# Small fp32 products of a state space mixer moved into tiles of the TensorE array, and a norm's last rows finished in pairs

## What is computed

```python
# even layer: [S5 complex-diagonal SSM (64 groups) | FoX forgetting attention (8 heads) | memory cross-attention (4 heads)]
# odd layer:  [latent attention (8 heads) | native sparse attention (8 heads) | memory cross-attention (4 heads)]
# h = h + W_out . concat_i( branch_i(RMSNorm(h)) * silu(gate_i) ), inputs and gates from ONE projection; one final RMSNorm

def s5_mixer(u, lam_re, lam_im, log_dt, b_re, b_im, c_re, c_im, d_skip, w_glu):
    ...
    bu_re = jnp.einsum('gpc,blgc->blgp', bb_re, uf)
    bu_im = jnp.einsum('gpc,blgc->blgp', bb_im, uf)
    ...
    _, _, xr, xi = lax.associative_scan(combine, (a_re, a_im, bu_re, bu_im), axis=1)
    y = (jnp.einsum('gcp,blgp->blgc', c_re.astype(f32), xr)
         - jnp.einsum('gcp,blgp->blgc', c_im.astype(f32), xi)
         + d_skip.astype(f32) * uf).reshape(B_, L, S5_WIDTH)
    z = jax.nn.gelu(y)
    z = z * jax.nn.sigmoid(z @ w_glu.astype(f32))

def rms_norm(x, g):
    y = xf * lax.rsqrt(jnp.mean(xf * xf, axis=-1, keepdims=True) + RMS_EPS)
```

## Time and profile before

| | |
|---|---|
| median of three runs | 2323.07 us (2321.97 to 2323.17) |
| profiled execution | 2319.24 us, its span 2317.6 us |
| PE busy | 2274.8 us (98%) |
| DVE, ACT, POOL busy | 1000.0, 825.0, 378.2 us |
| mean granted clock of TensorE | 0.997 |

### The profile page before, as it was taken

How to read it: one execution, slowest core, us unless ns; L and a number is a source line. 1 busy time by engine, 2 the same in 40 slices (tenths; PEclk the granted TensorE clock), 3 DMA queues, 4 the chain that set the end, 5 groups by cost and what they waited for, 6 DMA issues and landing times.

```text
span 2317.6 us, 30543 instructions
## 1 busy us (share of the span) xinstructions
PE 2274.8 (98%) x11765; PEld 1854.3 (80%) x11765; DVE 1000.0 (43%) x1875; ACT 825.0 (36%) x1467; POOL 378.2 (16%) x635
## 2 busy tenths in 40 slices
PE   7999999999999999999989999999999999999998
PEld 7888888888888877888878777888887866778886
DVE  4632454444432246553353442341122346666534
ACT  6533233333332434432342222322222443555323
POOL 1626112111110011110010001100000254121100
PEclk9999999999999999999999999999999999999999
DMA  7645434443445336654344446435533664454532
GB/s 278 205 143 139 122 106 120 119 119 111 124 115 186 110 111 202 201 193 132 91 151 138 131 140 223 133 118 164 158 109 98 210 212 159 142 193 154 204 108 94
DMA packets 165513, 345.62 MB, mean 149 GB/s; under 512 B 20639, under 2 KB 31215, under 8 KB 162947
## 3 DMA queue, kind: packets, MB, share of 16 engines
q1 hardware_dynamic: 106832, 188.51, 27.2%
q0 software_dynamic: 29840, 98.44, 13.3%
q10 hardware_dynamic: 28707, 56.84, 6.8%
HBM read 279.89 MB, written 63.83 MB: 148 GB/s over the span
## 4 chain that ended last, share of the span: by engine, by line
PE 96%; DVE 1%; ACT 1%; issue 1%; DMA 0%; SPq 0%; ACTq 0%; DVEq 0%
PE PS L241 78%; PE PS L1672 3%; PE PS L2338 2%; PE PS L1661 2%; PE PS L291 1%; PE PS L2235 1%; PE PS L548 1%; PE PS L1098 1%; PE PS L1094 1%; PE PS L1421 1%; PE PS L2198 1%; PE PS L1987 1%; PE PS L2231 1%; PE PS L1843 1%; PE PS L1071 1%
## 5 line engine op out<-in xcount | busy, mean ns | idle before, releaser
L241 PE MATMUL PS<-A,wsp 128*128 128x512 f32 (+2 forms) x5184 | 1160.6, 384 | 1.5 <-ACT stage L344 1.2
L241 PEld LDWEIGHTS PS<-A,wsp 128*128 128x128 f32 (+1 forms) x5184 | 942.3, 188 | 197.4 <-issue 8.6
L210 DVE TENSOR_TENSOR wsp<-wraw,wsp 128x1024 fp32r<-128x1024 f32 (+1 forms) x358 | 432.8, 1210 | 1025.9 <-ACT wsp L203 1024.9
L241 PE MATMUL PS<-wsp,A 128*128 128x512 f32 x2928 | 748.9, 400 | 4.2 <-DVE stage L1743 2.3
L203 ACT ACTIVATE wsp<-wraw 128x1024 fp32r<-128x1024 f32 (+1 forms) x358 | 372.2, 1042 | 988.8 <-PE PS L241 958.2
L241 PEld LDWEIGHTS PS<-wsp,A 128*128 128x128 f32 x2928 | 530.6, 189 | 104.7 <-issue 7.6
L344 ACT ACTIVATE stage<-PS 128x512 f32<-128x512 f32 (+1 forms) x150 | 87.0, 586 | 130.7 <-PE PS L241 126.0
L1708 ACT ACTIVATE S<-PS 128x256 f32<-128x256 f32 (+3 forms) x160 | 62.8, 393 | 123.3 <-PE PS L1661 122.4
L1672 PEld LDWEIGHTS PS<-S 128*128 128x128 f32 x640 | 92.5, 191 | 11.9 <-issue 2.4
L1716 ACT ACTIVATE S<-PS,stats 128x256 f32<-128x256 f32 (+3 forms) x160 | 74.6, 466 | 75.2 <-DVE stats L1753 63.1
L1672 PE MATMUL PS<-S 128*128 128x128 f32 x640 | 94.7, 275 | 1.2 <-issue 1.1
(11 more groups left out here) (337 smaller groups left out, 1743.1 us busy)
## 6 DMA issues: line engine op xcount, KB each, us to landing
wraw<-in_even_w_in_dram SPq DMA_DIRECT2D x112, 512.0 KB, 3.7
wraw<-in_odd_w_in_dram SPq DMA_DIRECT2D x88, 512.0 KB, 3.6
wraw<-in_w_out_dram SPq DMA_DIRECT2D x80, 512.0 KB, 3.7
wraw<-in_mem_w_kv_dram SPq DMA_DIRECT2D x32, 512.0 KB, 4.3
yO<-stage ACTq DMA_DIRECT2D x12, 1024.0 KB
yE<-stage ACTq DMA_DIRECT2D x10, 1024.0 KB
S<-yO POOLq DMA_DIRECT2D x36, 256.0 KB, 3.9
hA<-stage ACTq DMA_DIRECT2D x8, 1024.0 KB
```

The lines of the kernel that those rows point to most:

```text
L210: nc.vector.tensor_tensor(wsp[:, q, 1, :, 0:j["cols"]], wraw[:, q, :, 0:j["cols"]], wsp[:, q, 0, :, 0:j["cols"]].bitcast(F32), ALU.subtrac ...
L241: mm = nc.tensor.matmul(dst, lhs, rhs, start=(s == 0 and kk == 0 and i == 0), stop=(s == j["spc"] - 1 and kk == 1 and i == 2))
```

## The change

In the mixer: `pe_k` takes the small operand `exc` (32 columns) as weights and BP as moving operand, four column tiles of 32 after each other; K comes out turned, so ACT copies it (`act_kt`), and PE transposes it after slot 2 (`pe_kt`). `pe_x` makes products of 64 weight columns and 64 moving columns in two column halves of the array, into one bank. `pe_y` writes e = 0 to partitions 0 to 63 and e = 1 to 64 to 127 of bank 7 and stands as one block after slot 6. `pe_yt` transposes tiles of 128 rows x 64 columns in place of 64 x 128; the output to HBM goes in eight DMAs in place of one. ACT evacuates BU and Yn with one instruction each in place of two. Waits count along.

In the norm: two row tiles share one root; DVE and ACT scale row 0 and part of row 1 while the last bank is being filled; three parts of ACT's come after its first four tiles.

```diff
+        def act_row_square(act, v, t):
 
             act.wait_ge(banks_free, v["out"]["bank0"] + 13 + t)
             act.wait_ge(sq_done, v["sq0"] + 9 + t)
             nc.scalar.activation(s_tile(14336 + 512 * t), hrows[:, t, 3 * COLS:D], ACT.Square, accum_out=sqp[:, t, 3:4]).then_inc(sq_done, 1)
-            act.wait_ge(rms_step, v["step0"] + 4 * t + 1)
-            nc.scalar.activation(small[:, 8 + t:9 + t], small[:, 4 + t:5 + t], ACT.Sqrt).then_inc(rms_sqrt, 1)
-            act.wait_ge(row_root, v["row0"] + t + 1)
-
-        def dve_row_root(dve, v, t):
-
-            step = v["step0"] + 4 * t
-            dve.wait_ge(sq_done, v["sq0"] + 13 + t)
-            ssq, var, root, r0, r1, r = (small[:, 4 * i + t:4 * i + t + 1] for i in range(6))
-            nc.vector.tensor_reduce(ssq, sqp[:, t, :], AX, ALU.add).then_inc(row_sum, 1)
-            dve.wait_ge(row_sum, v["row0"] + t + 1)
+
+        def act_row_root(act, v, i):
+
+            t0, t1 = v["rows"] * i, v["rows"] * (i + 1)
+            act.wait_ge(rms_step, v["step0"] + 4 * i + 1)
+            nc.scalar.activation(small[:, 8 + t0:8 + t1], small[:, 4 + t0:4 + t1], ACT.Sqrt).then_inc(rms_sqrt, 1)
+            act.wait_ge(row_root, v["row0"] + i + 1)
...
+            dve.wait_ge(sq_done, v["sq0"] + 12 + t1)
+            ssq, var, root, r0, r1, r = (small[:, 4 * k + t0:4 * k + t1] for k in range(6))
+            nc.vector.tensor_reduce(ssq, sqp[:, t0:t1, :], AX, ALU.add).then_inc(row_sum, 1)
...
-            nc.vector.tensor_scalar(r1, r0, r0, var, ALU.mult, ALU.mult).then_inc(rms_step, 1)
+            if v["rows"] == 1:
+                nc.vector.tensor_scalar(r1, r0, r0, var, ALU.mult, ALU.mult).then_inc(rms_step, 1)
+            else:
+                nc.vector.tensor_tensor(r1, r0, r0, ALU.mult).then_inc(row_square, 1)
+                dve.wait_ge(row_square, i + 1)
+                nc.vector.tensor_tensor(r1, r1, var, ALU.mult).then_inc(rms_step, 1)
...
-                pe.wait_ge(rows_ok, {(0, 0): 2, (0, 4): 3, (1, 0): 8, (2, 0): 12, (2, 4): 13}[v["k"], k])
-            if (v["k"], k) in ((0, 0), (0, 4), (2, 2), (2, 8)):
-                pe.wait_ge(rows_act, {(0, 0): 1, (0, 4): 2, (2, 2): 6, (2, 8): 7}[v["k"], k])
+                pe.wait_ge(rows_ok, {(0, 0): 2, (0, 4): 3, (1, 0): 8, (2, 0): 11, (2, 4): 13}[v["k"], k])
+            if (v["k"], k) in ((0, 0), (0, 4), (2, 0), (2, 8)):
+                pe.wait_ge(rows_act, {(0, 0): 1, (0, 4): 2, (2, 0): 4, (2, 8): 7}[v["k"], k])
...
         def pool_y_out(pool, m):
 
             pool.wait_ge(y_ev, m + 1)
-            pool.dma_start(yS[m * P:(m + 1) * P, :], yT).then_inc(y_out, 16)
+            for e in range(2):
+                for j_ in range(4):
+                    row = m * P + 32 * j_ + 16 * e
+                    pool.dma_start(yS[row:row + 16, :], yT[16 * j_:16 * j_ + 16, e].rearrange("p n t -> p (n t)")).then_inc(y_out, 16)
...
-                pe.wait_ge(yn_ev, 2 * m)
-            for j_ in range(4):
-                for i in range(2):
-                    mm = nc.tensor.matmul(PS[:, 7, 32 * j_:32 * j_ + 32], BP[:, i, j_].rearrange("p s c -> p (s c)"), exc[:, i, j_, :],
+                pe.wait_ge(yn_ev, m)
+            for i in range(2):
+                for j_ in range(4):
+                    mm = nc.tensor.matmul(PS[32 * j_:32 * j_ + 32, 7, 0:128], exc[:, i, j_, :], BP[:, i, j_].rearrange("p s c -> p (s c)"),
                                           start=(i == 0), stop=(i == 1))
-            mm.then_inc(set_pe, 1)
+            mm.then_inc(k_pe, 1)
+
+        def act_kt(act, m):
+
+            act.wait_ge(k_pe, m + 1)
+            if m:
+                act.wait_ge(set_pe, 3 * m)
+            nc.scalar.activation(KT, PS[:, 7, 0:128], ACT.Copy).then_inc(kt_ev, 1)
+
+        def pe_kt(pe, m):
+
+            pe.wait_ge(kt_ev, m + 1)
+            nc.tensor.transpose(PS[:, 7, 128:256], KT, ident[:, :]).then_inc(set_pe, 1)
...
-                    mm = nc.tensor.matmul(PS[:, 4 + i, j_ * P:j_ * P + P], WT[:, i, j_, :], US[:, 2 * j_:2 * j_ + 2, :], start=True, stop=True)
+                    for e in range(2):
+                        q = slice(64 * e, 64 * e + 64)
+                        mm = nc.tensor.matmul(PS[q, 4, 256 * i + 64 * j_:256 * i + 64 * j_ + 64], WT[:, i, j_, q], US[:, 2 * j_ + e, :],
+                                              start=True, stop=True)
...
-                src = PS[q, 4:6, :].rearrange("p i (j e n) -> p i j e n", j=4, e=2)[:, :, :, e, :]
-                nc.scalar.activation(BU[q, :, :, :], src, ACT.Copy).then_inc(x_ev, 1)
+            nc.scalar.activation(BU, PS[:, 4, :].rearrange("p (i j n) -> p i j n", i=2, j=4), ACT.Copy).then_inc(x_ev, 1)
...
-            for j_ in (2 * half, 2 * half + 1):
-                dst = [PS[0:64, 6 + e, j_ * P:j_ * P + P] for e in range(2)]
+        def pe_y(pe, m):
+
+            pe.wait_ge(k_ev, 2 * (m + 1))
+            pe.wait_ge(wo_step, 6 * (m + 1))
+            pe.wait_ge(m_in, 128 * (m + 1))
+            pe.wait_ge(r_step, 9 * (m + 1))
+            for j_ in range(4):
+                dst = [PS[64 * e:64 * e + 64, 7, j_ * P:j_ * P + P] for e in range(2)]
                 for e in range(2):
                     nc.tensor.matmul(dst[e], US[:, 2 * j_ + e, :], MT[:, 2 * j_ + e, :], start=True, stop=False)
                 for i in range(2):
                     for e in range(2):
                         q = slice(e * 64, e * 64 + 64)
                         mm = nc.tensor.matmul(dst[e], stS[q, i, j_, 0:64], WO[q, i, j_].rearrange("p s c -> p (s c)"), start=False, stop=(i == 1))
-                        if i == 1 and j_ % 2 == 1:
-                            mm.then_inc(y_pe, 1)
+            mm.then_inc(y_pe, 1)
...
-                mm = nc.tensor.transpose(PS[:, 4, (7 - t) * 64:(8 - t) * 64], Yn[:, t, :], ident[0:64, 0:64])
+                mm = nc.tensor.transpose(PS[0:64, 4 + t // 4, t % 4 * P:t % 4 * P + P], Yn[:, 7 - t, :], ident[:, :])
...
+                if s == 2 and m < 8:
+                    pe_kt(pe, m)
+                if s == 6 and m < 8:
+                    pe_y(pe, m)
...
                 if s == 4 and m < 8:
+                    act_kt(act, m)
...
-                act_row_root(act, NORMS[2], t)
+            act_row_square(act, NORMS[2], 0)
+            act_row_square(act, NORMS[2], 1)
+            act_row_root(act, NORMS[2], 0)
+            act_row_square(act, NORMS[2], 2)
+            act_part(act, 0, 1024, D)
+            act_row_square(act, NORMS[2], 3)
+            act_row_root(act, NORMS[2], 1)
+            act_part(act, 2, 0, 512)
+            act_tiles(act, NORMS[2], range(4))
+            for t in range(1, 4):
                 act_part(act, t, 1024, D)
-            act_row_root(act, NORMS[2], 3)
-            act_part(act, 3, 256, 512)
-            act_tiles(act, NORMS[2], range(4))
-            act_part(act, 3, 1024, D)
             act_split(act, O1, 2)
             act_tiles(act, NORMS[2], (4, 5))
...
-                dve_out_row(dve, OUT0B, 3, 16, t)
-                dve_row_root(dve, NORMS[2], t)
-                dve_part(dve, t, 0, 1024)
+            dve_out_row(dve, OUT0B, 3, 16, 0)
+            dve_out_row(dve, OUT0B, 3, 16, 1)
+            dve_row_root(dve, NORMS[2], 0)
+            dve_out_row(dve, OUT0B, 3, 16, 2)
+            dve_part(dve, 0, 0, 1024)
             dve_out_row(dve, OUT0B, 3, 16, 3)
-            dve_row_root(dve, NORMS[2], 3)
-            dve_part(dve, 3, 0, 256)
+            dve_part(dve, 1, 0, 1024)
+            dve_row_root(dve, NORMS[2], 1)
+            dve_part(dve, 3, 0, 512)
             dve_tiles(dve, NORMS[2], range(4))
+            dve_part(dve, 2, 512, 1024)
             dve_part(dve, 3, 512, 1024)
             dve_split(dve, O1, 2)
             dve_tiles(dve, NORMS[2], (4, 5))
...
```

More of the change, by code:

```diff
@@ L388, in build @@
         junk = PS[:, 4:8, :]
-        NORMS = [dict(tiles=2, g=2, k=0), dict(tiles=4, g=0, k=1), dict(tiles=4, g=1, k=2, out=OUT0B, sq0=6, step0=10, root0=2, row0=0),
-                 dict(tiles=4, k=3, out=OUT1B, sq0=22, step0=26, root0=6, row0=4)]
+        NORMS = [dict(tiles=2, g=2, k=0), dict(tiles=4, g=0, k=1), dict(tiles=4, g=1, k=2, out=OUT0B, sq0=6, step0=10, root0=2, row0=0, rows=2),
+                 dict(tiles=4, k=3, out=OUT1B, sq0=22, step0=18, root0=4, row0=2, rows=1)]
         scaled = S[:, 8192:16384].rearrange("p (t d) -> p t d", t=4)
@@ L651, in build @@
         KS = high(128).rearrange("p (g c) -> p g c", g=8)
+        KT = high(128)
+        k_pe, kt_ev = sem("k_pe"), sem("kt_ev")
         kD = dram("kD", (8, 16, 8, 16, 16))
@@ L1078, in act_x @@
                 act.wait_ge(r_step, 9 * m)
-            for e in range(2):
-                q = slice(e * 64, e * 64 + 64)
-                src = PS[q, 4:6, :].rearrange("p i (j e n) -> p i j e n", j=4, e=2)[:, :, :, e, :]
-                nc.scalar.activation(BU[q, :, :, :], src, ACT.Copy).then_inc(x_ev, 1)
-        def pe_y(pe, m, half):
-            if half == 0:
-                pe.wait_ge(k_ev, 2 * (m + 1))
```

(31 more changed lines are left out.)

48 lines of the change are left out of this document (25 added, 23 removed).

## The result

The change takes the median from 2322.52 us (four runs on the same chip) to **2300.81 us** (2300.41 to 2301.95): ratio 0.9907, 95% interval 0.9896 to 0.9919. The forecast was 2311.5 with a range of 2302 to 2319, so the sign was right and the size about half of what came: 21.7 us were saved, 11.6 were forecast.

The account below looks back on a forecast made before the run. TensorE (PE), busy 98% of the span, was taken as the bound. Mixer -1.16 us per m, eight times, is 9.3; with 2.3 at the second norm 11.6, giving a median of 2311.5 us, range 2302 to 2319.

Parts of the forecast that it names:

- `pe_x` +0.28: Mixer: 32 smaller passes in place of 16, bound by weight loads, take 2.15 us per m against 1.87.
- `pe_y` -0.79: Mixer: MT products pair, 8 rounds in place of 16, as one block; 4.21 us per m, saving 0.79.
- `pe_k` -0.97: Mixer: 32-column weights in four column tiles take 0.85 us per m, saving 0.97.
- `pe_kt`: Mixer: the one added transpose costs 0.21 us per m.
- `pe_yt`: Mixer: eight transposes of 128 rows in the full array form cost 0.97 us per m against 0.86, so +0.11.
- rival 2: Mixer: packing weaker, `pe_k` two-wide and `pe_yt` in 64-column form, 2316.7 us; 2323.7 with two passes as well; chance 0.09.
- Rival 1: Mixer: loads into column tiles are free, 1.17 us less per m, 9.4 in all, giving 2302 us; chance 0.12.
- Rival 3: `pe_y`: state products in one bank no longer pair, +14.0 us, giving 2325.5, or 2338 with exposed loads; chance 0.11.
- Rival 4: Mixer: the K chain comes late, costing 8 us per us beyond 10 us of growth; 2327 us at 12; chance 0.04.
- The norm's mechanism: Second norm: shared roots and earlier scaling of rows shorten PE's standstill of 6.21 us, gaining 2.3 us.
- the lower of its two bounds: Second norm: the clock falls and returns at its old times, dense work runs at half and gives back 1.2; gain 1.1 us.
- The upper bound of 2.8: Second norm: the shorter gap doesn't make the clock fall and the transposes take half; gain 2.8 us.

Follow-up runs that it names:

- `pe_x` undone: Kernel after, with the products of `pe_x` back at 128 weight and 128 moving columns and ACT evacuating in two; 2304.32 us, ratio 0.9920 to the kernel before.
- the norm's part alone: Kernel before with only the second norm's part of the change, the mixer's stages left old; 2320.95 us, ratio 0.9993 to the kernel before.
- `pe_y` grouped: Kernel after, with all MT products of `pe_y` ahead of all state products, three changes of array form in place of nine; 2292.79 us, ratio 0.9876.
- the held clock: Kernel after, with 36 idle transposes of the identity into an unused bank in the second norm's gap; 2299.49 us, ratio 0.9906 to the kernel before.
- the mixer's part alone: Kernel before with only the mixer's part of the change, the norm's helpers and order left old; 2302.36 us, ratio 0.9911 to the kernel before.
- the step of 16 bytes: Kernel after, with the weight columns of `pe_x` stored 16 bytes apart and XL left alone; 2311.33 us in a single execution.
- the step of 32 bytes: Kernel after, with `pe_x` weight columns stored 32 bytes apart and those of L2225 (L2198 before) next to each other; 2308.87 us in a single execution.

## Why the prediction was wrong

**The step that failed** is "Row halves load at once, column halves share: 128 columns in two tiles cost what 128 columns in one do." It explained 107 against 50 ns by the tile's place in the array. The cause was the layout of the weights: L2198 reads columns 128 bytes apart. Shown from both sides: `pe_x` with a step takes 2.19 us per m (449.62 - 436.53 - 10.90), close to the forecast's 2.15; L2225 without one exposes 53 ns. (That closeness is in part luck: the forecast added 0.11 for the first load to changes of form of 0.15 that already hold it.) That "it is the same shape and type as the new `pe_x`" was true of the weight tile and not enough: the moving tile has 256 columns there and 64 here, and a row of the trace doesn't show the access pattern; the code at that line does.

The forecast lay 10.7 us above the median: 9.5 are the mixer (8 x 1.19), the norm gives 1.3 back (1.0 came in this trace, 2.3 was forecast), and 2.5 are left.

Point by point:
- `pe_x` +0.28 was forecast, -0.67 came: 0.95 x 8 = 7.6 us of the miss.
- `pe_y` -0.79 was forecast, -1.05 came: the +0.22 for four doubled loads fell away by the same error, 0.26 x 8 = 2.1 us. The pairing of MT products and the 0.15 per change of form held.
- `pe_k` -0.97 was forecast, -1.07 came; the 0.11 for its first load was the same error, 0.024 in the profile, and counted twice, since the 0.15 per change of form already holds a first load. `pe_kt` held. `pe_yt` held (one pass each, no change of form), and so a part of rival 2 fell. The Trainium skill ("TensorEngine Tiling (Array Packing)", Restrictions) says that column tiling disables the transpose mode for fp32; these transposes of 64 columns, at 0.109 each and in the full form, show no loss by it.
- `pe_set` grew by 0.09, which had been put at nothing. Counted from start to start it carries the change of form ahead of `pe_k`: with `pe_x` undone, the slot ahead of that stage loses the same 0.09.
- Rival 1 (free loads) happened in its sum, 1.19 per m against its 1.17, though the loads aren't free: 48 ns of them show once, ahead of the first pass, and the rest are covered at 0.058 per pair.
- Rival 3 did not happen. State passes of two row tiles in one bank start in pairs as before: 0.65 us for eight (0.38/7 = 0.054 each). The Trainium skill (the same page, Gotcha 1) has it that different row tiles can't access one bank at a time; where they write different partitions, as here, the trace shows no turn-taking.
- Rival 4 did not happen: PE shows no idle time ahead of `pe_y`.
- The norm's mechanism was right, 2.08 us of standstill against 2.3 (the second root came 3.27 us after its row was taken up, not 3.05). In the kernel after, the lower of its two bounds held (1.1; 1.0 came), since the half clock then lies on O1's first slot. That is one execution's outcome: by the same count, from L291's block to the second slot, the same norm gave 1.2 (the norm's part alone), 2.2 (`pe_x` undone), 2.1 and 0.9 (steps of 32 and 16 bytes) and 1.6 us (`pe_y` grouped), as the half clock lay. So the 2.3 taken for the sum was a choice between the bounds with no row behind it, but no impossible one. The upper bound of 2.8, for a clock that doesn't fall, has no working in the prediction; the held clock showed it, 2.8.
- That the changed kernel's median would stand 3.8 us above its profiled time, as before, was an unsaid guess: it stands 1.1 below. That fits the clock in the attention stages, full in the profiled execution before and not in the one after; the other runs have no trace. With the measured terms (18.8 and 1.0) the same sum would have been 2303.3. Of the 2.5 to the measured 2300.8, 0.55 are the kernel before itself (2322.52 over four runs, 2323.07 over three), and the rest is within the noise: 19.8 us saved is a ratio of 0.9915, inside the interval.

## What to carry to other kernels

When a duration is taken over from another line of a trace, compare the access patterns in the code, not the shapes alone: fp32 weights whose columns lay 16 or 32 bytes apart made `pe_x` run at half the rate, and that alone decided whether the stage gained or lost. Small fp32 products packed into column tiles are worth it when their weights are contiguous, and they should be grouped by array form, since a change of form costs 0.15 us. What a shorter standstill ahead of dense work pays depends on what the 1.2 GHz stretch then covers (the same standstill gave 0.9 to 2.2 us here), so look at what runs during it, before and after, and in more than one execution.

## What the runs showed of the hardware

- A load of 64 fp32 weight columns, exposed: 48 to 53 ns contiguous; 112 with a step of 32 bytes; 107 and more with a step of 128 bytes. Covered, its record is 138 ns contiguous and 218 at steps of 16 or 32 bytes, and pairs of loads and passes into the two column tiles follow each other by 0.058 us contiguous and 0.120 with the step of 32 bytes.
- Work that changed nothing in the attention stages still moves their clock. In executions of otherwise equal stages there are two stretches of 3.4 us at 1.2 GHz (the kernel after, the mixer's part alone, the step of 16 bytes; 3.2 us lost), one of 6.8 (the norm's part alone, `pe_x` undone, the step of 32 bytes; 2.4 to 2.7 lost) or none (the kernel before twice, the held clock alone and with the grouping, `pe_y` grouped). What decides it is open. Runs of one and the same kernel spread by 5.9 us (2319.31 to 2325.23), with mean clocks from 0.998 to 0.995; a smaller difference between single executions can't be read as the work of an edit without the traces side by side.
- At the norm the half clock around the standstill of 4.13 us lasted 6.8 us in the kernel after, `pe_y` grouped and the step of 16 bytes, and 3.4 us with `pe_x` undone and the step of 32 bytes.
